# Four blocks on one core: three wide experts in 96 slots on 32-column quarters, a ring of six, and half of a layer's modulation rows elsewhere

## The reference

```python
logits = (t @ router); vals, idx = lax.top_k(logits, 2); wts = softmax(vals)
for e in range(8):
    out = out + comb[:, e:e + 1] * ((silu(t @ w1[e]) * (t @ w3[e])) @ w2[e])
```

## Time and profile before

| | |
|---|---|
| runs | 2904.4, 2899.6, 2903.25 us; median 2903.25 |
| profiled execution | 2905.51 us, of which 2903.8 us span |
| TensorE busy | 2848.0 us, 98% |
| weight loads busy | 2308.5 us, beside the matmuls |
| VectorE, ScalarE, GpSimd busy | 942.8, 516.1, 93.7 us |
| DMA | 705.72 MB, mean 243 GB/s |
| experts | from 781.9 us (first gather) to 1778.5 us (end of the last scatter) |

### The profile page before, as it was taken

How to read it: one execution, slowest core, us unless ns; L and a number is a source line. 1 busy time by engine, 2 the same in 40 slices (tenths; PEclk the granted TensorE clock), 3 DMA queues, 4 the chain that set the end, 5 groups by cost and what they waited for, 6 DMA issues and landing times.

```text
span 2903.8 us, 39304 instructions
## 1 busy us (share of the span) xinstructions
PE 2848.0 (98%) x16450; PEld 2308.5 (79%) x16450; DVE 942.8 (32%) x2168; ACT 516.1 (18%) x1019; POOL 93.7 (3%) x181
## 2 busy tenths in 40 slices
PE   7999999999899999999999999989999999999999
PEld 6789889878888388568738856778898897789888
DVE  2654332354311011111102103465255325643330
ACT  3331000323200000000000002232221023331210
POOL 0000110000000000000000000000001100000000
PEclk9999999999899999999999999999999999999999
DMA  8436765424299989979998995233366543233432
GB/s 366 182 145 225 267 249 223 162 104 172 105 426 425 393 323 423 398 316 409 413 384 329 424 391 230 110 116 116 145 226 248 221 189 118 91 114 146 176 126 95
DMA packets 71311, 705.72 MB, mean 243 GB/s; under 512 B 7904, under 2 KB 8160, under 8 KB 31584
## 3 DMA queue, kind: packets, MB, share of 16 engines
q1 hardware_dynamic: 45648, 610.40, 53.0%
q0 software_dynamic: 25488, 92.81, 8.5%
HBM read 702.13 MB, written 1.05 MB: 242 GB/s over the span
## 4 chain that ended last, share of the span: by engine, by line
PE 70%; DVE 2%; ACT 1%; issue 0%; DVEq 0%; ACTq 0%
PE psum L922 28%; PE psum L1150 14%; PE psum L1161 7%; PE psum L1190 7%; PE psum L1187 4%; PE psum L937 4%; PE psum L1121 1%; PE psum L986 1%; PE psum L1201 1%; PE psum L1072 1%; PE psum L946 1%; PE psum L1036 1%; PE psum L1138 1%; PE psum L978 0%; PE psum L993 0%; PE psum L1057 0%
## 5 line engine op out<-in xcount | busy, mean ns | idle before, releaser
L922 PE MATMUL psum<-hT,ring 128*128 128x256 f32 x4544 | 994.6, 380 | 0.0
L922 PEld LDWEIGHTS psum<-hT,ring 128*128 128x128 f32 x4544 | 859.9, 190 | 122.2 <-ACT work L1442 3.3
L1150 PE MATMUL psum<-work,ring 128*128 128x128 f32 x3584 | 409.8, 275 | 0.0
L1150 PEld LDWEIGHTS psum<-work,ring 128*128 128x128 f32 x3584 | 407.6, 193 | 1.7 <-issue 1.5
L922 PE MATMUL psum<-work,ring 128*128 128x256 f32 x1624 | 353.4, 379 | 0.0
L922 PEld LDWEIGHTS psum<-work,ring 128*128 128x128 f32 x1624 | 308.1, 190 | 42.5 <-ACT work L1311 0.7
L1161 PE MATMUL psum<-ring,work 128*64 128x256 f32 x1792 | 205.7, 382 | 0.0
L1190 PE MATMUL psum<-ring,work 128*128 128x512 f32 x448 | 200.7, 599 | 0.0
L1190 PEld LDWEIGHTS psum<-ring,work 128*128 128x128 f32 x448 | 82.5, 190 | 115.2 <-issue 115.2
L1161 PEld LDWEIGHTS psum<-ring,work 128*64 128x64 f32 x1792 | 123.7, 137 | 63.4
L2100 DVE CUSTOM_DVE_ANT_0 mod_in<-mod_in,c_rows,cols 128x1024 f32<-128x1024 f32 x128 | 160.1, 1278 | 41.8 <-DMA mod_in<-in_mods 41.8
(11 more groups left out here) (228 smaller groups left out, 1917.0 us busy)
## 6 DMA issues: line engine op xcount, KB each, us to landing
ring<-in_m SPq DMA_DIRECT2D x112, 2048.0 KB, 11.2
ring<-in_m SPq DMA_DIRECT2D x64, 1792.0 KB, 9.3
ring<-in_w_in SPq DMA_DIRECT2D x46, 2048.0 KB, 8.2
mod_in<-in_mods POOLq DMA_DIRECT2D x176, 512.0 KB, 6.9
ring<-in_up SPq DMA_DIRECT2D x22, 2048.0 KB, 8.0
ring<-in_f SPq DMA_DIRECT2D x11, 2048.0 KB, 8.3
ring<-in_down SPq DMA_DIRECT2D x16, 1408.0 KB, 6.7
ring<-in_w_o SPq DMA_DIRECT2D x8, 2048.0 KB, 8.2
```

What stands on the lines that cost most here:

```text
L922: last = mm(gbank(it["bank"])[:, j, :], wt[:, k, col0 + j * P:col0 + (j + 1) * P], rhs[:, k0 + k, :], start=(n == 0), stop=(n == total - 1))
L1150: last = mm(o[:, j * P:(j + 1) * P], wt[:, k, j * P:(j + 1) * P], picked[0][:, k, :], start=(k == 0), stop=(k == DK - 1))
```

## The change

1. Wide experts of rank two to four (pairs 1 to 3 of 0 to 3) get 96 slots. In `up` their tokens become stationary, 32 at a time on a 32-column quarter, and 256 weight columns move (`thirds`). Each of the 28 groups of 256 weight columns needs three quarters, so 84 quarters make 21 units of four; a chunk lasts one and a half units. Their results have tokens on partitions and are turned like the narrow expert's. `pair_steps` fixes the order of wide and narrow units, `bank_numbers` numbers their banks. `down` and `scatter` use 96 columns and rows. Pair 0 stays as it was.
2. The ring has six slots in the experts (`ROUND_RING`), two of them in the work area. Outside the experts it has four.
3. Half of layer 3's modulation rows (24 of 48, `EARLY_MODS`) are computed in the first FFN, with a second constants row (`second_rows`) that is loaded and put through Silu at the start. In the pairs six rows are left instead of twelve, behind every second narrow unit.
4. The router allows three passes, with two more small operations on VectorE.

```diff
-    put("width", np.where(np.arange(8) % 2, 64.0, 128.0).astype(np.float32)[None, :])
+    put("width", np.where(np.arange(8) % 2, 64.0, np.where(np.arange(8), 96.0, 128.0)).astype(np.float32)[None, :])
...
-            plan.extend(spread(items, adas(0, 40, 48) + adas(1, 0, 28)))
+            plan.extend(spread(items, adas(0, 40, 48) + adas(1, 0, 28) + adas(2, 0, 12)))
...
-            slots = {0: adas(1, 28, 32), 1: adas(1, 32, 36)}
+            slots = {0: adas(1, 28, 36) + adas(2, 12, 14), 1: adas(2, 14, EARLY_MODS)}
...
+def pair_steps(q):
+
+    steps, done = [], 0
+    for i in range(FE_U):
+        if q == 0:
+            steps.append(("w", i))
+        else:
+            while done < THIRDS and (4 * done + 3) // 6 <= i:
+                steps.append(("w", done))
+                done += 1
+        steps.append(("n", i))
+    return steps
...
+        blocks = [ring[:, i, :] for i in range(RING)] + [work[:, off + i * SLOT:off + (i + 1) * SLOT]
+                                                         for i in range(ROUND_RING - RING)]
...
+                sp.dma_start(second_rows, arrays["c_rows"][1:2].to_broadcast([P, D])).then_inc(
+                    inputs_loaded, w.step(of="inputs", by=16))
...
-                                slot = g % RING
+                                slot = g % ROUND_RING
...
-                                if g >= RING:
-                                    sp.wait_ge(tensor_round, r.at("r_used", g - RING))
+                                if g >= ROUND_RING:
+                                    sp.wait_ge(tensor_round, r.at("r_used", g - ROUND_RING))
...
+                def thirds(n):
+                    b = bank_at[q, "w", n]
+                    o, jobs, used = bank_of(r, b), [], []
+                    for m in range(4 * n, 4 * n + 4):
+                        f, part = m // 3, m % 3
+                        g = q * PAIR_CHUNKS + 2 * (f // 2)
+                        jobs.append((part, f % 2, block(r, g).rearrange("p (k n) -> p k n", n=512)))
+                        if m % 6 == 5:
+                            used.append(("r_used", g))
+                    for k in range(DK):
+                        if n == 0 and k % 4 == 0:
+                            pe.wait_ge(scalar_round, r.at("r_picked", q, 0, k // 4))
+                        for j, (part, side, wt) in enumerate(jobs):
+                            last = mm(o[32 * j:32 * j + 32, 0:T], picked[0][:, k, 32 * part:32 * part + 32],
+                                      wt[:, k, side * T:(side + 1) * T], start=(k == 0), stop=(k == DK - 1))
+                    last.then_inc(tensor_round, r.step(("r_bank", b), *used))
...
+                for kind, i in pair_steps(q):
+                    if kind == "n":
+                        narrow(i)
+                    elif q == 0:
+                        wide(i)
+                    else:
+                        thirds(i)
+                    if i and (kind == "n" or q):
+                        turn(kind, i - 1)
+                if q:
+                    turn("w", THIRDS - 1)
+                turn("n", FE_U - 1)
...
+                                elif q:
+                                    last = mm(outs[0][0:96, :], hid_flat[:, 96 * f:96 * f + 96], wt[:, k, :],
+                                              start=(f == 0), stop=(f == 27))
...
-                V.tensor_tensor(key, key, con("width"), ALU.is_gt).then_inc(*then())
+                V.tensor_tensor(over, key, con("width"), ALU.is_gt).then_inc(*then())
+                V.scalar_tensor_tensor(out=key, in0=key, scalar=0.5, in1=con("width"), op0=ALU.mult,
+                                       op1=ALU.is_gt).then_inc(*then())
...
+                    if kind == "n" and i % 2 and i // 2 < ROUND_MODS:
+                        ada_column(i // 2)
```

More of the change, by code:

```diff
@@ L615, in all_of, with bank_numbers, put @@
         return self.n * whole + whole
+def pair_steps(q):
[9 more added lines that the diff above has]
+    return steps
+def bank_numbers():
+    at, n = {}, 0
+    def put(*key):
+        nonlocal n
+        at[key] = n
+        n += 1
+    for q in range(PAIRS):
+        for kind, i in pair_steps(q):
+            put(q, kind, i)
+        for half in range(2):
+            for kind in "wn":
+                put(q, "down_" + kind, half)
+        for kind in "wn":
+            for u in range(4):
+                put(q, "back_" + kind, u)
+    return at
 def build(nc, arrays, out, book, ccols, ccons):
@@ L697, in build @@
         off += 3 * T
-        hid_s = region(off, 2, P)
-        off += 2 * P
+        hid_s = [region(off, 2, P), region(off + 2 * P, 2, P)]
+        off += 4 * P
         hid_e = [region(off, D_FE // P, P), region(off + D_FE, D_FE // P, 64)]
+        hid_flat = work[:, off:off + D_FE]
         off += D_FE + D_FE // 2
@@ L709, in build @@
         route = work[:, off + 608:off + 640].rearrange("p (f k) -> p f k", k=8)
-        assert off >= hb + 2560 and off + 640 <= WN
+        assert off >= hb + 2560
+        off += 640
+        blocks = [ring[:, i, :] for i in range(RING)] + [work[:, off + i * SLOT:off + (i + 1) * SLOT]
+                                                         for i in range(ROUND_RING - RING)]
+        assert off + (ROUND_RING - RING) * SLOT <= WN
+        second_rows = work[:, WN - D:WN]
+        assert WN - D >= tmp1 + 2048 + 1536
         order = sb("order", [P, 8], I32)
@@ L792, in build @@
         rounds = {"round_PE": tensor_round, "round_ACT": scalar_round, "round_DVE": vector_round}
-        round_loaded = [sem(f"round_slot{i}_loaded") for i in range(RING)]
+        round_loaded = [sem(f"round_slot{i}_loaded") for i in range(ROUND_RING)]
         round_mod_loaded = [sem(f"round_mod{i}_loaded") for i in range(MODS)]
@@ L1130, in gather, with block, wide @@
                 last.then_inc(tensor_round, r.step(("r_weights", q)))
+            def block(r, g):
+                pe.wait_ge(round_loaded[g % ROUND_RING], r.at("r_loaded", g))
+                return blocks[g % ROUND_RING]
             def up(r, q):
[L1134 to L1142, removed]
+                def wide(i):
+                    g, b = q * PAIR_CHUNKS + 2 * i, bank_at[q, "w", i]
                     o = bank_of(r, b)
-                    pe.wait_ge(round_loaded[g % RING], r.at("r_loaded", g))
-                    wt = ring[:, g % RING, :].rearrange("p (k n) -> p k n", n=512)
+                    wt = block(r, g).rearrange("p (k n) -> p k n", n=512)
                     for j in range(4):
@@ L1482, in pair @@
+                    if i and (kind == "n" or q):
+                        hid(kind, i - 1)
+                if q:
+                    hid("w", THIRDS - 1)
+                hid("n", FE_U - 1)
                 for half in range(2):
-                    for n in range(2):
-                        b = q * PAIR_BANKS + 2 * (FE_U + half) + n
+                    for n, kind in enumerate("wn"):
+                        b, rows = bank_at[q, "down_" + kind, half], 96 if q and not n else P
                         act.wait_ge(tensor_round, r.at("r_bank", b))
-                        A(y_e[n][:, half * 512:(half + 1) * 512], psum[:, b % GBANKS, :], ACT.Copy).then_inc(
+                        A(y_e[n][0:rows, half * 512:(half + 1) * 512], psum[0:rows, b % GBANKS, :], ACT.Copy).then_inc(
@@ L1990, in router @@
                 own()
-                V.tensor_tensor(key, key, con("width"), ALU.is_gt).then_inc(*then())
+                V.tensor_tensor(over, key, con("width"), ALU.is_gt).then_inc(*then())
+                V.scalar_tensor_tensor(out=key, in0=key, scalar=0.5, in1=con("width"), op0=ALU.mult,
+                                       op1=ALU.is_gt).then_inc(*then())
                 V.tensor_reduce(small[:, 84:86], E, AX.X, ALU.add).then_inc(*then())
                 own()
+                V.tensor_tensor(key, key, over, ALU.add).then_inc(*then())
+                V.reciprocal(small[:, 86:88], small[:, 84:86]).then_inc(*then())
+                own()
                 V.tensor_reduce(small[:, 144:145], key, AX.X, ALU.max).then_inc(*then())
-                V.reciprocal(small[:, 86:88], small[:, 84:86]).then_inc(*then())
                 own()
```

142 lines of the change are left out of this document (77 added, 65 removed).

## The result

| | before | after |
|---|---|---|
| median | 2902.86 us (4 runs, 2899.6 to 2904.4) | 2861.43 us (4 runs, 2859.4 to 2865.6) |
| ratio | | 0.986, 95% interval 0.9845 to 0.9876 |
| profiled execution | 2905.51, span 2903.8 | 2865.60, span 2863.9 |

A forecast was written before the change was run, and what follows sets the result against it. TensorE, busy 98%, was taken as the bound, DMA 7% behind. 2905.5 - 57.1 + 3 + 8.3 + 2.6 + 0.4 = 2862.7 us; with the profiled execution 2.3 over its median, 2860 us, range 2848 to 2874 (2894 with rivals).

The forecast's parts named there:

- The quarter unit: Up phase of pairs two to four: a unit takes 3.60 us plus a 0.26 us turn, saving 57.1 us.
- rival B: Quarter units: surplus counts per record, so a unit takes 3.8 to 4.25 us, gain 45 to 16 us; chance 0.10.
- Rival A: Quarter units: instruction issue limits, so a unit takes 7.15 us and the kernel 3081 us; chance 0.12.
- DMA in the pairs: Later pairs: weight transfer fits over a pair, with 1 us of waiting each, 3 us in all.
- the head start: Up phase of later pairs: six ring slots leave about 14.8 us of transfer ahead, just covering 10.2 us short.
- the prediction's own shortage: Up phase of later pairs: 135.1 us of work against 145.3 us of transfer, 10.2 us short.
- Rival C: Later pairs: head start fails and DMA binds, 5 to 15 us waiting a pair, 2882 us; chance 0.12.
- The stall in the first FFN: Down units' moved modulation rows delay an eviction: TensorE waits 8.3 us at the sums, then loses 2.6 us to half clock.
- the landing of the tenth row: First FFN, behind a down unit: the tenth modulation row lands 3.5 us after its buffer is asked for, ending at 477.9.
- The walk: VectorE's queue in the first FFN's down units: 1.28 us a row, landings 9.5 or 3.5 us, third eviction 15.1 us late.
- Two router operations: Router: two more small VectorE operations before the first gather, some 0.2 us each, 0.4 us in all.
- The up units of the first FFN: Twelve more modulation rows there, 48 instead of 36 over 22 units, cost nothing.

The follow-up runs named there:

- experiment 4: Changed kernel with each quarter matmul split into two of 128 moving columns, 128 load and matmul pairs a unit: 2901.71 us (one run).
- Experiment 6: Changed kernel without quarters, all four wide experts on 128 moving tokens, six slots and early modulation rows kept: 2918.78 us, ratio 1.0046.
- experiment 8: Changed kernel with each quarter matmul split into four of 64 moving columns, 256 load and matmul pairs a unit: 3195.22 us (one run).
- Experiments 3 and 2: Both edit the changed kernel. 3: layer 3's modulation rows back in the pairs, twelve each, none early, 2864.98 us; 2: four ring slots in the experts, 2932.69 us.

## Why the prediction was right, point by point

**The quarter unit.** Booked 3.60 us and 0.26, measured 3.59 and 0.26. Booked 57.1 us for three pairs, and less the 3 us of waiting 54.1; measured 58.4, waits included. Some 0.2 us a pair come from down, where a step of both experts takes 9.75 instead of 9.79 us with 96 stationary columns; I had left that at 0 with 1 us either way. Some 0.4 us a pair come from a shorter wait for VectorE at the end of up (0.6 us instead of 1.0). The surplus of 0.19 us counts per unit and not per record, which puts rival B aside; experiment 4 holds 128 record pairs in 3.63 us. Experiment 6 gives 57.3 of these 58.4 us to the quarters; six slots and fewer rows bring the other 1.1. Rival A fell by the same row. The page that I weighed (the Trainium skill, "TensorE: Matmul & The Clock Gate", Part 1) gives 25 ns as the least distance of matmul starts, or 62 with hardware decode off. This case's trace has 53 ns in the quarter unit and 15.5 ns a record within stretches of experiment 8, so the 62 don't bind here, and records of different quarters go below the 25 too. There page and trace differ, and the trace decides.

**DMA in the pairs.** Booked 3 us of waiting, measured some 1.9. The number was near and the account behind it was not; that is luck. I wrote that a pair has 12 us of transfer time to spare, and that four slots would leave 4.9 of the 10.2 us covered. Experiments 3 and 2 say otherwise: 3.1 MB more cost 7.5 us at once, and four slots cost 24.3 us a pair, not 5.3. The step that fails is the head start. By the prediction's own shortage (17.6 us in experiment 3, of which 7.5 are waited for) six slots cover about 10 us and not 14.8; it just suffices. Two things are behind it. DMA stands still for 14 us of every pair, while the ring is full and up to the end of the second quarter unit (2 GB/s from 1056.5 to 1070.3), and these are the 12 us that I took to be spare. Outside it DMA runs near 426 GB/s, in down too (427 over 78 us, not 409). So 91.2 MB take 214 us of a pair of 229.1, 94.4 MB take 222 of 236.6 (experiment 3): both lose 15 us against the ceiling. With five slots it is 20 us, with four 39. And a held wide chunk blocks not one slot but every load behind it. The changed kernel's 229.1 us is where both bounds meet. Rival C, by its sign of 5 us a pair and more, was one slot or some four modulation rows a pair away.

**The stall in the first FFN.** Booked 8.3 and 2.6 us, measured 14.1 and 2.0. Right in place and kind, 5.2 us too small. The term that was mis-sized is the landing of the tenth row. The walk had its buffer asked for at 474.3, some 0.3 us before the unit's end frees two weight chunks, and booked 3.5 us. With the 1.17 us by which this kernel was late, it was asked for just as the walk says, and ahead of the chunks; but it took as long as if it had gone behind them, and VectorE got it at 485.1 instead of 477.9:
```profile
475.58 0.53 POOL L2318 DMA_DIRECT2D mod_in<-in_mods  x1 [2.44 <-DVE ada L2197]
...
475.78 0.33 SPq L878 DMA_DIRECT2D ring<-in_f  x1
...
DMA to landing us min/median/max: 9.4/9.4/9.4
```
From there on the rows were 4 us behind the walk and more, at the end some 7. Three rows instead of two were held up by the 2 MB chunks, the first of them asked for 0.8 us before the chunks. VectorE waited for rows eleven times, not five. A queue whose service time is 3.5 or 9.5 us by so little has to be booked with both.

**The rest.** Two router operations: booked 0.4, measured 0.3 (the gather waits 5.1 instead of 4.8 us). The up units of the first FFN: booked 0, measured 0.1. Not booked: 1.1 us at the start and some 1.9 us at the router, where the same matmuls ran at the lower clock level. The fourth of the first modulation chunks took 3.64 us against 2.53, and the router's first logits 3.42 against 1.85. Both follow idle stretches of TensorE in both kernels. Neither is the change's: in the twelve traces of this document the first mixer starts between 32.2 and 36.8 us, and from the router's first logits to the first gather it takes 15.9 to 18.4 us, in no order with the edits. This is as much as the runs of one kernel scatter (2859.4 to 2865.6). One token pass stayed one.

Against the sum the experts came out 4.3 us better, the stall 5.2 us worse and the rest 2.0 us worse: 2.9 us in the span. In medians it is 1.4 us, since the profiled execution lay 4.2 us over its median and that of before 2.3. The point was nearer than its parts, which is luck: errors of 4 and 5 us cancelled. The prediction also gives its upper end twice, 2874 in the sum and 2894 in the chances, where rivals B and C (2883, 2882) are counted in; 2861.4 lies inside both.

## What to carry to other kernels

Work that is moved onto an idle engine is free only up to the next eviction on that engine whose bank someone waits for: count how many operations fit before it, with the slow transfer time, and place no more (18 early rows in the up units, five in the down units and one in the mixer made no wait in the trace; 12 and 12 cost 16 us). When a faster engine meets a transfer bound, the depth of the ring decides: in order of issue a chunk that is held long blocks all loads behind it, and one slot too few can cost more than the whole gain (58 us gained, 71 lost with four slots). The spare transfer time of a stage is its period minus the bytes at the ceiling rate minus the pauses in which the ring is full: here 229 - 214 - 14, so 1 us. The pauses end only when the first slot comes free. Instructions are traffic too: before cutting matmuls into shorter ones, look how many of them a unit needs.

## What the runs showed of the hardware

- Four matmuls with 32 stationary columns on the four quarters of the array run at the full rate: 64 records of 256 moving columns in 3.59 us, 16 slots of 0.213 us and 0.18 us. Halving the moving columns leaves a unit at 3.63 us.
- TensorE can't be fed with short matmuls without end. At 128 instructions (64 matmul records with their loads) in 3.59 us nothing stops; at 256 in the same time there are stops of up to 2.0 us; at 512, stops of up to 5.0 us every 128 or so matmul records, and the pair takes 346.9 instead of 229.0 us. Nearly idle DMA engines shorten them by over a third, from 222.9 to 139.5 us. They end 1.1 to 1.6 us after a 16 KB packet of the instruction queue (some 250 instructions), and in the pairs two packets never started less than 3.3 us apart.
- The 16 DMA engines bring 426 GB/s with 2 MB and with 1.8 MB loads, but only as long as the ring has a free slot: 15, 20 and 39 us of a pair were lost against that rate with six, five and four slots.
- A modulation row of 0.5 MB lands 3.5 us after its issue on an idle DMA, and 9.2 to 12.4 us after it beside two 1.4 or 2 MB chunks (longest: asked for at 497.56, used at 510.12), even if it was issued 0.2 us before them (475.58).
